# Reading two weight matrices in wide halves instead of quarters while expert rows stream in

## The chip, the core and the metric

The kernel runs on one core of one Trainium2 chip. The metric is the device time of one execution in microseconds (us), lower is better. Time before: 3602.56 us, the median of 3 runs (3600.56 to 3604.57).

## What is computed

Two layers of an encoder over 256 tokens of width 2048, all in float32. Layer 0 mixes tokens with latent attention, layer 1 with attention that has a forget gate (`fox`). After each mixer comes an expert layer (PEER): 8 query heads pick 16 experts each out of 16384 by two lists of 128 keys, so 128 expert rows of `u` and 128 of `v` (8 KB each) are fetched for every token.

```
def fox_mixer(h, w_in, b_f, g_q, g_k, w_o):
    z = h @ w_in                                   # 2048 x (4*2048 + 16)
    q, k, v, gate, f_logit = split(z)
    ...                                            # attention, 16 heads of 128
    return (o * sigmoid(gate)) @ w_o               # 2048 x 2048
def peer_ffn(h, w_q, sub_keys, u, v):
    q = x @ w_q                                    # 2048 x 2048
    scores = einsum('thcd,cnd->thcn', q, sub_keys)
    ...                                            # top 16 of each list, top 16 of the sums, softmax g
    a = gelu(einsum('tkd,td->tk', u[idx], x)) * g
    return einsum('tk,tkd->td', a, v[idx])
```

## The kernel before, in words

**Slots and windows.** The expert layer is a stream of 512 slots. One slot serves 128 tokens with one expert each: it gathers 128 rows of `u` and 128 rows of `v` (1 MB each). 128 slots are a window: window 0 and 1 are layer 0's token blocks 0 and 1, window 2 and 3 those of layer 1. For slot n, GpSimd (POOL) issues the gathers (L672 for `u`, L682 for `v`), VectorE (DVE) forms the dot products (L1967), ScalarE (ACT) applies gelu and gate and builds a diagonal matrix (L1396, L1400, L1405), TensorE (PE) adds `diag @ v` for 1536 columns to three PSUM banks (`accumulate`, L981) and DVE does the last 512 columns (L1978). `u` and `v` have a ring of 4 buffers each; a buffer is gathered into again when the slot four before is through.

**Jobs inside the slots.** Layer 1's mixer and the expert queries of layer 1, for one token block, are a "job" that is spread over the slots of a window: job 0 runs in window 1, job 1 in window 2. The place of every step is a slot number written out by hand; in each slot an engine first does the slot's expert work and then, in program order, what `job(b, at)` lists for that slot. All engines wait in order, so a step that has to wait holds up the engine's next slots.

**Weights in a job.** SyncE (SP) loads 98 pieces of 1 MB per job into a ring of 4 buffers (`stage`, taken in turn): a gain row, 64 pieces of the input matrix `fox_w_in`, 16 of the output matrix `fox_w_o`, a gain row, 16 of the query matrix `peer_w_q`. SP issues piece m when piece m-4 has been used (`staged`, L583). For the input matrix a piece is an *eighth*: 256 rows by 1024 columns (`stage_wide`, L601, so 4096 bytes of each row), and PE sums 1024 columns at once into banks 3 and 4 (`in_eighth`, L1033, matmuls L1045), one eighth per slot from slot 6 to 69. For `fox_w_o` and `peer_w_q` a piece is a *quarter*: 512 rows by 512 columns (`stage_quarter`, L597, 2048 bytes of each row), summed into one bank (`gemm_quarter`, L1024, matmuls L1030).

**Order around the change.** The output projection has four column tiles of four quarters, placed by `OUT_ORDER` at slots 70 to 73, 79 to 83, 85 to 91; a quarter needs the transposed attention outputs of its four heads (`ot_done`). Tile t is added to the residual by DVE one slot after its last quarter (`out_add`, L2071). At slot 93 (`FFN_AT`) ACT squares the residual, DVE normalises at 94 (`b_norm`, L1990; it uses the gain row and waits for its load), PE transposes at 95 and 96, ACT copies at 96 and 97. From slot 98 (`PQ_AT`) to 113 the 16 quarters of `peer_w_q` are summed, tiles alternating between banks 3 and 4; ACT copies tile i four slots after its start (`pq_copy`, L1543), PE transposes it, ACT copies that (L1550), PE multiplies by the keys, ACT stores the scores (L1556, last at slot 118). The first reader of the scores is DVE at slot 121 (`choose`, which waits for the first tile alone).

Of the kernel before, what the change touches and what calls it, by code (L numbers as in the profile page):

```python
# [26 lines left out]
ALU = mybir.AluOpType  # L27
# [7 lines left out]
P = 128  # L35
# [109 lines left out]
def hybrid_encoder(nc, x, positions, norm_mix_g, norm_ffn_g, mla_w_in, mla_g_qa, mla_w_qb, mla_g_kva,  # L145
                   mla_w_kvb, mla_g_q, mla_g_k, mla_w_o, fox_w_in, fox_b_f, fox_g_q, fox_g_k, fox_w_o,
                   peer_w_q, peer_sub_keys, peer_u, peer_v, inv_freq, out):
    with ExitStack() as ctx:
# [295 lines left out]
        def out_summed(job, t):  # L444
            return after(job, M_OUT + OUT_LOADS.index((t, 3)))

        def pq_summed(job, i):
            return after(job, M_PQ + 4 * i + 3)
# [31 lines left out]
        def _(sp):  # L480
# [114 lines left out]
            def stage_quarter(job, m, w, q, c0):  # L595
                r = staged(job, m)
                sp.dma_start(stage[:, r], w[:, 4 * q:4 * q + 4, c0:c0 + TILE]).then_inc(stage_full[r], 16)  # L597

# [102 lines left out]
        def _(pe):  # L701
# [283 lines left out]
            def b_transposes(b, ffn, quads):  # L985

                pe.wait_ge(bn_done, 2 * b + ffn + 1)
                if not ffn and quads[0] == 0:
                    if b == 0:

                        pe.wait_ge(match_done, PHEADS)
                    else:

                        pe.wait_ge(pq_evac, 4 * b)
                        pe.wait_ge(score_done, 4 * b)
                if ffn and quads[0] == 0:

                    pe.wait_ge(out_added, 4 * (b + 1))
# [25 lines left out]
            def gemm_quarter(job, m, q, bank, src):  # L1024

                r, turn = stage_of(job, m)
                pe.wait_ge(stage_full[r], 16 * (turn + 1))
                for c in range(4):
                    k = 4 * q + c
                    last = pe.matmul(psum[:, bank, :], src[:, k, :], stage[:, r, c, :], start=k == 0, stop=k == KC - 1)  # L1030
                last.then_inc(stage_used, 1)

            def in_eighth(b, i, e):  # L1033


# [4 lines left out]
                r, turn = stage_of(b, M_IN + 8 * i + e)  # L1040
                pe.wait_ge(stage_full[r], 16 * (turn + 1))
                for c in range(2):
                    k = 2 * e + c
                    for half in range(2):
                        last = pe.matmul(psum[:, 3 + half, :], b_xT[:, k, :], wide(r)[:, c, half * TILE:(half + 1) * TILE],  # L1045
                                         start=k == 0, stop=k == KC - 1)
                last.then_inc(stage_used, 1)
# [58 lines left out]
            def out_quarter(b, t, q):  # L1106

                if q == 0:
                    if t < 2:
                        pe.wait_ge(in_evac, 8 * b + 8)  # L1110
                    elif t == 2:
                        pe.wait_ge(s_masked, HEADS * (b + 1))
                    else:
                        pe.wait_ge(og_done, HEADS * (b + 1))
                pe.wait_ge(ot_done, HEADS * b + 4 * q + 4)
                gemm_quarter(b, M_OUT + OUT_LOADS.index((t, q)), q, OUT_BANKS[t], b_attnT)

            def pq_quarter(b, i, q):

                if q == 0 and i < 2:  # L1120
                    pe.wait_ge(bt_done, 8 * b + 8)
                elif q == 0:
                    pe.wait_ge(pq_evac, 4 * b + i - 1)
                gemm_quarter(b, M_PQ + 4 * i + q, q, 3 + i % 2, b_xT)

            def pq_turned(b, i):

                number = 4 * b + i
                pe.wait_ge(pq_evac, number + 1)
                if i:  # L1130
                    pe.wait_ge(pqt_done, number)
                for c in range(4):
                    last = transpose(psum[:, 5, c * P:(c + 1) * P], b_v[:, c * P:(c + 1) * P])
                last.then_inc(pqt_full, 1)
# [12 lines left out]
            def job(b, at):  # L1147
# [25 lines left out]
                if at in OUT_ORDER:  # L1173
                    out_quarter(b, *OUT_ORDER[at])
                if FFN_AT + 2 <= at < FFN_AT + 4:
                    b_transposes(b, 1, range(2 * (at - FFN_AT - 2), 2 * (at - FFN_AT - 1)))
                for i in range(4):
                    if at == PQ_AT + 4 * i + 5:
                        pq_turned(b, i)
                    if at == PQ_AT + 4 * i + 7:  # L1180
                        pq_scores(b, i)
                if PQ_AT <= at < PQ_AT + 16:
                    pq_quarter(b, (at - PQ_AT) // 4, (at - PQ_AT) % 4)
# [27 lines left out]
        def _(act):  # L1211
# [235 lines left out]
            def b_square(b, ffn):  # L1447

                if ffn:
                    act.wait_ge(out_added, 4 * (b + 1))  # L1450
# [87 lines left out]
            def pq_copy(b, i):  # L1538

                number = 4 * b + i  # L1540
                act.wait_ge(stage_used, pq_summed(b, i))
                act.wait_ge(pqt_full, number)
                nc.scalar.activation(b_v[:, 0:TILE], psum[:, 3 + i % 2, :], ACT.Copy).then_inc(pq_evac, 1)  # L1543
# [14 lines left out]
            def job(b, at):  # L1558
# [28 lines left out]
                if FFN_AT + 3 <= at < FFN_AT + 5:  # L1587
                    b_copies(b, 1, range(2 * (at - FFN_AT - 3), 2 * (at - FFN_AT - 2)))
                for i in range(4):
                    lag = at - (PQ_AT + 4 * i)  # L1590
                    if lag == 4:
                        pq_copy(b, i)
                    if lag == 6:
                        pq_turned(b, i)
                    if lag == 8:
# [40 lines left out]
        def _(dve):  # L1636
# [430 lines left out]
            def out_add(b, t):  # L2067

                dve.wait_ge(stage_used, out_summed(b, t))
                cols = resid[:, b, t * TILE:(t + 1) * TILE]  # L2070
                V.tensor_tensor(cols, psum[:, OUT_BANKS[t], :], cols, ALU.add).then_inc(out_added, 1)  # L2071

            def job(b, at):
# [22 lines left out]
                if OUT_ORDER.get(at - 1, (0, 0))[1] == 3:  # L2096
# [57 lines left out]
```

## Time and profile before

| what | value |
|---|---|
| median of the runs | 3602.56 us |
| the profiled execution, its own time | 3597.09 us |
| span of the profile (first to last instruction) | 3595.0 us |
| mean granted TensorE clock | 0.913 of full |
| busy: PE, DVE, ACT, POOL | 80%, 57%, 26%, 41% of the span |
| bytes moved | 1345.35 MB, 374 GB/s over the span |
| of them gathers (POOL's queue) | 1073.81 MB |
| of them SP's loads | 269.99 MB |

The profiled execution is 5.5 us under the median. Times in all views are from the start of the span. "DMA share" is the mean busy share of the core's 16 DMA engines; packets of two queues overlap a little, so a full queue reads 1.01 to 1.02. In the wait views the name before the arrow is the engine that sat idle, the one behind it the work that ended the wait; "issue" is idle time for which the profile shows no releaser. "Us to landing" is the time from SP's or POOL's issue of a transfer to its last byte.

### The profile page before, as it was taken

To read this page: it belongs to the slowest core of one execution; us is meant where nothing else is said; L and a number is where in the kernel's file an instruction comes from. 1 tells how busy PE (TensorE), PEld (TensorE's weight loads), DVE (VectorE), ACT (ScalarE), POOL (GpSimd) and SP (SyncE) were. 2 spreads that over 40 slices of the span, in tenths; PEclk is the share of its full clock that TensorE was granted. 3 is DMA by queue.
4 is the path that set the end of the run, shared out by engine and by line. 5 is a ranking of instruction groups with operands and counts; after the bars stand their busy time and mean duration, and the time that the engine had idled before them with its cause. 6 is when DMAs were issued, how large, how long until landed. Compare 5 with 4: busy or idle time off the path is not lost.

```text
span 3595.0 us, 26702 instructions
## 1 busy us (share of the span) xinstructions
PE 2877.5 (80%) x7322; PEld 1355.1 (38%) x7322; DVE 2034.9 (57%) x3584; ACT 945.4 (26%) x2349; POOL 1456.3 (41%) x1065
## 2 busy tenths in 40 slices
PE   7888977777786888888788788998988867776766
PEld 6445743333332433333333233443433322222222
DVE  2333156666667554555464655455546467677765
ACT  3334322222222223323221222332322122222221
POOL 4002545555655322222343532322234355555554
PEclk8877988898998999999998899999999988888888
DMA  4212599999999999999999999999999989999998
GB/s 144 82 61 89 195 386 416 416 412 415 418 419 421 418 417 417 417 417 413 409 406 400 408 418 417 417 417 417 413 412 410 400 362 421 421 421 421 422 420 360
DMA packets 262853, 1345.35 MB, mean 374 GB/s; under 512 B 27200, under 2 KB 48192, under 8 KB 130368
## 3 DMA queue, kind: packets, MB, share of 16 engines
q0 software_dynamic: 147456, 1073.81, 72.2%
q1 hardware_dynamic: 115264, 269.99, 19.9%
q8 instruction: 56, 0.92, 0.1%
q14 instruction: 77, 0.63, 0.0%
HBM read 1341.62 MB, written 2.10 MB: 374 GB/s over the span
## 4 chain that ended last, share of the span: by engine, by line
DMA 61%; PE 20%; issue 12%; POOL 3%; DVE 2%; ACT 1%; SPq 1%; DVEq 0%; POOLq 0%; ACTq 0%
DMA room<-in_peer_v_dram,index 51%; PE psum L981 11%; DMA wbuf<-in_fox_w_o_dram 5%; DMA wbuf<-in_peer_w_q_dram 4%; PE psum L1030 2%; PE psum L1045 2%; POOL room L672 1%; PE psum L744 1%; PE psum L745 1%; PE psum L746 1%; POOL room L682 1%; DMA room<-in_peer_u_dram,index 1%; DVE resid L1978 0%; SPq L539 0%; POOL w_low L656 0%
## 5 line engine op out<-in xcount | busy, mean ns | idle before, releaser
L981 PE MATMUL psum<-room,diag 128*128 128x512 f32 x3072 | 1605.6, 664 | 554.2 <-DMA room<-in_peer_v_dram,index 493.9
L1967 DVE CUSTOM_DVE_ANT_0 room<-room,normed 128x2048 f32<-128x2048 f32 x512 | 1172.8, 2291 | 613.7 <-DMA room<-in_peer_u_dram,index 609.4
L682 POOL DMA_INDIRECT room<-in_peer_v_dram,index x512 | 749.4, 1464 | 1083.3 <-PE psum L981 1050.1
L981 PEld LDWEIGHTS psum<-room,diag 128*128 128x128 f32 x3072 | 603.6, 208 | 1497.0 <-issue 1239.8
L672 POOL DMA_INDIRECT room<-in_peer_u_dram,index x512 | 590.7, 1154 | 729.5 <-DVE dots L1967 482.4
L1396 ACT ACTIVATE acts<-dots 128x1 f32<-128x1 f32 x512 | 103.4, 202 | 1765.6 <-DVE dots L1967 1765.2
L1978 DVE SCALAR_TENSOR_TENSOR resid<-room,acts,resid 128x512 f32<-128x512 f32 x512 | 384.2, 750 | 306.6 <-DMA room<-in_peer_v_dram,index 236.8
L1045 PE MATMUL psum<-wbuf,normedT 128*128 128x512 f32 x1024 | 463.6, 595 | 0.0
L1030 PE MATMUL psum<-wbuf,normedT 128*128 128x512 f32 x512 | 272.4, 682 | 83.4 <-DMA wbuf<-in_peer_w_q_dram 41.8
L1045 PEld LDWEIGHTS psum<-wbuf,normedT 128*128 128x128 f32 x1024 | 188.9, 190 | 214.7 <-issue 212.0
L656 POOL TENSOR_TENSOR w_low<-wbuf,w_high 128x2048 fp32r<-128x2048 f32 (+1 forms) x28 | 113.9, 4080 | 304.4 <-ACT w_high L1251 304.4
L1405 ACT ACTIVATE diag<-ident,acts 128x128 f32<-128x128 f32 x512 | 205.5, 401 | 48.3 <-ACT acts L1400 1.5
L1030 PEld LDWEIGHTS psum<-wbuf,normedT 128*128 128x128 f32 x512 | 108.5, 219 | 225.0 <-issue 183.6
L1400 ACT ACTIVATE acts<-acts,gates 128x1 f32<-128x1 f32 x512 | 150.8, 295 | 16.6
L873 PE MATMUL psum<-wbuf,room 128*128 128x384 f32 (+1 forms) x256 | 119.4, 605 | 0.7 <-ACT room L1283 0.7
L920 PE MATMUL psum<-normedT,wbuf 128*128 128x256 f32 x448 | 106.0, 379 | 0.0
L920 PEld LDWEIGHTS psum<-normedT,wbuf 128*128 128x128 f32 x448 | 85.5, 191 | 36.5 <-issue 27.8
L1396 ACT ACT_TABLE_LOAD x74 | 94.9, 1283 | 1.3
L706 PE MATMUL psum<-ident,room 128*128 128x128 f32 x192 | 46.6, 341 | 31.8 <-DVE room L1714 14.0
L1251 ACT ACTIVATE w_high<-wbuf 128x2048 fp32r<-128x2048 f32 (+1 forms) x28 | 47.5, 1702 | 80.6 <-DMA wbuf<-in_mla_w_o_dram 52.1
L873 PEld LDWEIGHTS psum<-wbuf,room 128*128 128x128 f32 x256 | 50.8, 216 | 37.8 <-issue 30.1
L1811 DVE CUSTOM_DVE_ANT_0 room<-psum,mask_mla 128x128 f32<-128x128 f32 (+1 forms) x32 | 11.5, 358 | 93.8 <-PE psum L816 91.9
(199 smaller groups left out, 1800.8 us busy)
## 6 DMA issues: line engine op xcount, KB each, us to landing
wbuf<-in_fox_w_in_dram SPq DMA_DIRECT2D x128, 1024.0 KB, 12.5
wbuf<-in_fox_w_o_dram SPq DMA_DIRECT2D x32, 1024.0 KB, 31.9
wbuf<-in_peer_w_q_dram SPq DMA_DIRECT2D x32, 1024.0 KB, 28.2
wbuf<-in_mla_w_o_dram SPq DMA_DIRECT2D x16, 1024.0 KB, 5.1
wbuf<-in_peer_w_q_dram SPq DMA_DIRECT2D x32, 512.0 KB, 9.1
wbuf<-in_mla_w_in_dram SPq DMA_DIRECT2D x8, 1024.0 KB, 8.3
wbuf<-in_mla_w_kvb_dram SPq DMA_DIRECT2D x32, 256.0 KB, 3.4
room<-in_peer_u_dram,index POOLq DMA_INDIRECT x512, 16.6
```

The costliest lines, as they stand in the source:

```text
L672: pool.indirect_dma_start(u_ring[:, r, :], None, u_table, bass.IndirectOffsetOnAxis(index[:, number % 2, s:s + 1], 0)).then_inc(u_full[r], 16)
L682: pool.indirect_dma_start(v_ring[:, r, :], None, v_table, bass.IndirectOffsetOnAxis(index[:, number % 2, s:s + 1], 0)).then_inc(v_full[r], 16)
L873: last = pe.matmul(gbank(gh, b)[:, 0:n], (cqT, ckvT)[t][:, k, b * P:(b + 1) * P], wbuf[:, wh, k, 0:n], start=k == 0, stop=k == RC - 1)
L920: last = pe.matmul(psum[:, 4 + c, 0:T], pq_tile[:, r, k, c * P:(c + 1) * P], normedT[:, k, :], start=k == 0, stop=k == KC - 1)
L981: mm = pe.matmul(psum[:, q, :], diag[:, r, :], v_ring[:, r, q * TILE:(q + 1) * TILE], start=at == 0, stop=at == WINDOW - 1, skip_group_che ...
L1030: last = pe.matmul(psum[:, bank, :], src[:, k, :], stage[:, r, c, :], start=k == 0, stop=k == KC - 1)
L1045: last = pe.matmul(psum[:, 3 + half, :], b_xT[:, k, :], wide(r)[:, c, half * TILE:(half + 1) * TILE], start=k == 0, stop=k == KC - 1)
L1396: chain.step(nc.scalar.activation(acts[:, 0, r:r + 1], dots[:, r:r + 1], ACT.Gelu))
L1400: chain.step(nc.scalar.activation(acts[:, 1, r:r + 1], acts[:, 0, r:r + 1], ACT.Copy, scale=gates[:, number % 2, s:s + 1]))
L1405: nc.scalar.activation(diag[:, r, :], ident[:, :], ACT.Copy, scale=acts[:, 1, r:r + 1]).then_inc(diag_ready, 1)
L1967: V.tensor_tensor_reduce(u_ring[:, r, :], u_ring[:, r, :], normed[:, b, :], 1.0, 0.0, ALU.mult, ALU.add, dots[:, r:r + 1]).then_inc(dot_do ...
L1978: V.scalar_tensor_tensor(out=resid[:, b, PE_COLS:D], in0=v_ring[:, r, PE_COLS:D], scalar=acts[:, 1, r:r + 1], in1=resid[:, b, PE_COLS:D], ...
```

## The change

The 32 quarters of a job become 32 eighths, as the input matrix has them: 256 rows by 1024 columns, still 1 MB each, in eight steps per half of the matrix. The output projection's first half sums into banks 3 and 4, its second into 5 and 6. A half is added to the residual by one DVE instruction of 1024 columns; the two query halves both use banks 3 and 4, each copied by one ACT instruction of 1024 columns, and the transposes read that copy in two parts of 512 columns. The order is written anew: output eighths at slots 70 to 73, 79, 80, 83, 85 to 93; the norm and the queries start two slots later.

```diff
-FFN_AT = 93
-PQ_AT = 98
-OUT_ORDER = {70: (0, 0), 71: (0, 1), 72: (1, 0), 73: (1, 1), 79: (0, 2), 80: (1, 2), 81: (2, 0), 82: (2, 1),
-             83: (2, 2), 85: (3, 0), 86: (3, 1), 87: (0, 3), 88: (1, 3), 89: (2, 3), 90: (3, 2), 91: (3, 3)}
-OUT_BANKS = (3, 4, 6, 5)
+FFN_AT = 95
+PQ_AT = 100
+OUT_ORDER = {70: (0, 0), 71: (0, 1), 72: (0, 2), 73: (0, 3), 79: (0, 4), 80: (0, 5), 83: (0, 6), 85: (1, 0),
+             86: (1, 1), 87: (0, 7), 88: (1, 2), 89: (1, 3), 90: (1, 4), 91: (1, 5), 92: (1, 6), 93: (1, 7)}
+OUT_BANKS = (3, 5)
+def pq_at(i):
+    return PQ_AT + 8 * (i // 2) + 2 * (i % 2)
...
-                for m, (t, q) in enumerate(OUT_LOADS):
-                    stage_quarter(job, M_OUT + m, ow, q, t * TILE)
+                for m, (half, e) in enumerate(OUT_LOADS):
+                    stage_wide(job, M_OUT + m, ow, e, half * WIDE)
                 stage_gain(job, M_FFN, norm_ffn_g[1:2, :])
-                for t in range(4):
-                    for q in range(4):
-                        stage_quarter(job, M_PQ + 4 * t + q, qw, q, t * TILE)
+                for half in range(2):
+                    for e in range(8):
+                        stage_wide(job, M_PQ + 8 * half + e, qw, e, half * WIDE)
...
-            def gemm_quarter(job, m, q, bank, src):
+            def gemm_eighth(job, m, e, bank, src):
                 r, turn = stage_of(job, m)
                 pe.wait_ge(stage_full[r], 16 * (turn + 1))
-                for c in range(4):
-                    k = 4 * q + c
-                    last = pe.matmul(psum[:, bank, :], src[:, k, :], stage[:, r, c, :], start=k == 0, stop=k == KC - 1)
+                for c in range(2):
+                    k = 2 * e + c
+                    for half in range(2):
+                        last = pe.matmul(psum[:, bank + half, :], src[:, k, :], wide(r)[:, c, half * TILE:(half + 1) * TILE],
+                                         start=k == 0, stop=k == KC - 1)
                 last.then_inc(stage_used, 1)
...
+            def out_eighth(b, half, e):
+                if e == 0 and half == 0:
+                    pe.wait_ge(in_evac, 8 * b + 8)
+                elif e == 0:
+                    pe.wait_ge(s_masked, HEADS * (b + 1))
+                    pe.wait_ge(og_done, HEADS * (b + 1))
+                pe.wait_ge(ot_done, HEADS * b + 2 * e + 2)
+                gemm_eighth(b, M_OUT + OUT_LOADS.index((half, e)), e, OUT_BANKS[half], b_attnT)
+            def pq_eighth(b, half, e):
+                if e == 0 and half == 0:
+                    pe.wait_ge(bt_done, 8 * b + 8)
+                elif e == 0:
+                    pe.wait_ge(pq_evac, 2 * b + 1)
+                gemm_eighth(b, M_PQ + 8 * half + e, e, 3, b_xT)
...
+            def pq_copy(b, half):
+                act.wait_ge(stage_used, pq_summed(b, half))
+                act.wait_ge(pqt_full, 4 * b + 2 * half)
+                nc.scalar.activation(b_v, psum[:, 3:5, :].rearrange("p k n -> p (k n)"), ACT.Copy).then_inc(pq_evac, 1)
...
+            def out_add(b, half):
+                dve.wait_ge(stage_used, out_summed(b, half))
+                cols = resid[:, b, half * WIDE:(half + 1) * WIDE]
+                bank = OUT_BANKS[half]
+                V.tensor_tensor(cols, psum[:, bank:bank + 2, :].rearrange("p k n -> p (k n)"), cols,
+                                ALU.add).then_inc(out_added, 1)
```

In the new order PE transposes query part i at slot `pq_at(i) + 9` and multiplies it by the keys at +11; ACT copies a half at `PQ_AT + 8 * half + 8`, the transposed part at `pq_at(i) + 10` and the scores at +12 (slots 112, 114, 120, 122). `in_eighth` now calls `gemm_eighth` with the same matmuls as before. The other waits on `out_added` and `pq_evac` count two per job instead of four.

## Rows read from the trace of the kernel before

**Rows 1.** The page: DMA share (tenths) and rate, span in 40 slices.

```profile
DMA  4212599999999999999999999999999989999998
GB/s 144 82 61 89 195 386 416 416 412 415 418 419 421 418 417 417 417 417 413 409 406 400 408 418 417 417 417 417 413 412 410 400 362 421 421 421 421 422 420 360
```

**Rows 2.** Busy time, clock, DMA share and rate in stretches; first row names columns.

```profile
core 0: us, PE busy (x) PEld busy (x) DVE busy (x) ACT busy (x) POOL busy (x), PEclk, DMA share, GB/s
1190.00:1630.00 440.00, 381.46 (x943) 165.40 (x942) 230.31 (x443) 120.12 (x272) 115.47 (x117) 1.00 1.02 417
...
1640.00:1990.00 350.00, 289.12 (x681) 127.44 (x680) 181.44 (x297) 91.96 (x224) 121.93 (x96) 0.92 1.01 407
2540.00:2900.00 360.00, 305.86 (x761) 139.22 (x760) 189.90 (x308) 97.25 (x235) 133.60 (x100) 0.93 0.99 394
2980.00:3560.00 580.00, 408.23 (x693) 148.72 (x694) 407.90 (x607) 125.02 (x376) 324.14 (x232) 0.85 1.01 421
1792.00:1800.00 8.00, 6.97 (x15) 2.73 (x14) 5.33 (x16) 0.90 (x3) 1.93 (x2) 0.89 0.93 333
1928.00:1936.00 8.00, 8.00 (x20) 3.54 (x20) 5.64 (x6) 1.56 (x6) 3.85 (x2) 0.85 0.84 315
2828.00:2836.00 8.00, 8.00 (x20) 3.48 (x18) 5.67 (x6) 1.52 (x5) 3.77 (x2) 0.79 0.81 303
2884.00:2892.00 8.00, 8.00 (x19) 3.48 (x18) 3.49 (x4) 2.17 (x7) 2.27 (x1) 0.87 0.01 4
```

**Rows 3.** DMA queues, 1210 to 1620 us (eighths load): packets, MB, share of 16 engines.

```profile
q0 software_dynamic: 15632, 113.84, 66.9%
q1 hardware_dynamic: 14782, 57.01, 34.7%
```

**Rows 4.** DMA queues, 1650 to 1780 us (quarters load).

```profile
q0 software_dynamic: 5684, 41.38, 77.1%
q1 hardware_dynamic: 6161, 12.23, 25.0%
```

**Rows 5.** Line 1978, once a slot: 1190-1630, 1725-1770, 1838-1890, 2980-3560 us (count; durations; first, last start).

```profile
L1978 DVE SCALAR_TENSOR_TENSOR resid<-room,acts,resid x58: 746/752/753, 1191.0 to 1626.6; 128x512 f32<-128x512 f32 x58
...
L1978 DVE SCALAR_TENSOR_TENSOR resid<-room,acts,resid x7: 752/752/753, 1726.6 to 1765.2; 128x512 f32<-128x512 f32 x7
...
L1978 DVE SCALAR_TENSOR_TENSOR resid<-room,acts,resid x9: 750/752/753, 1838.3 to 1889.8; 128x512 f32<-128x512 f32 x9
...
L1978 DVE SCALAR_TENSOR_TENSOR resid<-room,acts,resid x116: 745/751/753, 2981.5 to 3558.6; 128x512 f32<-128x512 f32 x116
```

**Rows 6.** The page's DMA issues: count, KB each, median us to landing.

```profile
wbuf<-in_fox_w_in_dram SPq DMA_DIRECT2D x128, 1024.0 KB, 12.5
wbuf<-in_fox_w_o_dram SPq DMA_DIRECT2D x32, 1024.0 KB, 31.9
wbuf<-in_peer_w_q_dram SPq DMA_DIRECT2D x32, 1024.0 KB, 28.2
```

**Rows 7.** Who waited for whom, whole span: us in total, times, longest us.

```profile
DVE resid L1978 <- issue: 68.9, 8, 18.8
...
DVE resid L2071 <- PE psum L1030: 50.2, 6, 22.1
```

**Rows 8.** Timeline around 2880 us: start, us, engine, line, operation, idle before.

```profile
2880.33 6.54 PE L1030 MATMUL psum<-wbuf,normedT 128*128 128x512 f32 x8 [4.70 <-DMA wbuf<-in_peer_w_q_dram]
...
2886.91 0.60 ACT L1543 ACTIVATE wbuf<-psum 128x512 f32<-128x512 f32 x1 [10.64 <-PE psum L1030]
...
2889.72 2.55 POOL L682 DMA_INDIRECT room<-in_peer_v_dram,index  x1 [12.26 <-PE psum L981]
```

**Rows 9.** Single lines: count, duration ns min/median/max, first and last start.

```profile
L1484 ACT ACTIVATE share<-psum x8: 1024/1024/1027, 1236.7 to 2441.7; 128x1024 f32<-128x1024 f32 x8
...
L1543 ACT ACTIVATE wbuf<-psum x8: 597/597/601, 1876.8 to 2886.9; 128x512 f32<-128x512 f32 x8
...
L2071 DVE TENSOR_TENSOR resid<-psum,resid x8: 680/692/693, 1794.6 to 2719.8; 128x512 f32<-128x512 f32 x8
```

More of the change, by code:

```diff
@@ L442, in in_summed, with out_summed, pq_summed @@
             return after(job, M_IN + 8 * i + 7)
[L444 to L448, printed above, removed]
+        def out_summed(job, w):
+            return after(job, M_OUT + OUT_LOADS.index((w, 7)))
+        def pq_summed(job, w):
+            return after(job, M_PQ + 8 * w + 7)
         def psum_tile(n):
@@ L992, in b_transposes @@
                     else:
-                        pe.wait_ge(pq_evac, 4 * b)
+                        pe.wait_ge(pq_evac, 2 * b)
                         pe.wait_ge(score_done, 4 * b)
                 if ffn and quads[0] == 0:
-                    pe.wait_ge(out_added, 4 * (b + 1))
+                    pe.wait_ge(out_added, 2 * (b + 1))
                 for q in quads:
@@ L1039, in in_eighth @@
                     pe.wait_ge(in_evac, 8 * b + i)
[L1040 to L1047, printed above, removed]
+                gemm_eighth(b, M_IN + 8 * i + e, e, 3, b_xT)
             def qk_turned(b, g, kind, half):
@@ L1104, in out_turned @@
                 transpose(psum[:, 7, T:T + P], b_og[:, :]).then_inc(ot_full, 1)
[L1106 to L1120, printed above, removed]
+            def out_eighth(b, half, e):
[8 more added lines that the diff above has]
+                if e == 0 and half == 0:
                     pe.wait_ge(bt_done, 8 * b + 8)
-                elif q == 0:
-                    pe.wait_ge(pq_evac, 4 * b + i - 1)
-                gemm_quarter(b, M_PQ + 4 * i + q, q, 3 + i % 2, b_xT)
+                elif e == 0:
+                    pe.wait_ge(pq_evac, 2 * b + 1)
+                gemm_eighth(b, M_PQ + 8 * half + e, e, 3, b_xT)
             def pq_turned(b, i):
                 number = 4 * b + i
-                pe.wait_ge(pq_evac, number + 1)
+                pe.wait_ge(pq_evac, 2 * b + i // 2 + 1)
                 if i:
@@ L1132, in pq_turned @@
                 for c in range(4):
-                    last = transpose(psum[:, 5, c * P:(c + 1) * P], b_v[:, c * P:(c + 1) * P])
+                    at = i % 2 * TILE + c * P
+                    last = transpose(psum[:, 5, c * P:(c + 1) * P], b_v[:, at:at + P])
                 last.then_inc(pqt_full, 1)
@@ L1173, in job @@
                 if at in OUT_ORDER:
-                    out_quarter(b, *OUT_ORDER[at])
+                    out_eighth(b, *OUT_ORDER[at])
                 if FFN_AT + 2 <= at < FFN_AT + 4:
@@ L1177, in job @@
                 for i in range(4):
-                    if at == PQ_AT + 4 * i + 5:
+                    if at == pq_at(i) + 9:
                         pq_turned(b, i)
-                    if at == PQ_AT + 4 * i + 7:
+                    if at == pq_at(i) + 11:
                         pq_scores(b, i)
                 if PQ_AT <= at < PQ_AT + 16:
-                    pq_quarter(b, (at - PQ_AT) // 4, (at - PQ_AT) % 4)
+                    pq_eighth(b, (at - PQ_AT) // 8, (at - PQ_AT) % 8)
             def peer():
@@ L1449, in b_square @@
                 if ffn:
-                    act.wait_ge(out_added, 4 * (b + 1))
+                    act.wait_ge(out_added, 2 * (b + 1))
                 else:
@@ L1536, in out_copy @@
                 nc.scalar.activation(b_attnT[:, h, :], psum[:, 7, T:T + P], ACT.Copy).then_inc(ot_done, 1)
[L1538 to L1543, printed above, removed]
+            def pq_copy(b, half):
+                act.wait_ge(stage_used, pq_summed(b, half))
+                act.wait_ge(pqt_full, 4 * b + 2 * half)
+                nc.scalar.activation(b_v, psum[:, 3:5, :].rearrange("p k n -> p (k n)"), ACT.Copy).then_inc(pq_evac, 1)
             def pq_turned(b, i):
@@ L1588, in job @@
                     b_copies(b, 1, range(2 * (at - FFN_AT - 3), 2 * (at - FFN_AT - 2)))
+                for half in range(2):
+                    if at == PQ_AT + 8 * half + 8:
+                        pq_copy(b, half)
                 for i in range(4):
[L1590 to L1593, printed above, removed]
+                    if at == pq_at(i) + 10:
                         pq_turned(b, i)
-                    if lag == 8:
+                    if at == pq_at(i) + 12:
                         pq_scores(b, i)
@@ L2095, in job @@
                             qk_norm(b, g, kind)
-                if OUT_ORDER.get(at - 1, (0, 0))[1] == 3:
+                if OUT_ORDER.get(at - 1, (0, 0))[1] == 7:
                     out_add(b, OUT_ORDER[at - 1][0])
```

7 lines of the change are left out of this document (removed).

## The prediction, made before the changed kernel ran

> **What bounds the kernel now.** I read the page's DMA slices first [rows 1]: from the sixth slice to the end nearly all stand at 9, so the expert stream is bound by bytes, and no engine's busy time matters as long as the DMA engines have work. The rate, though, isn't the same everywhere: 417 in the slices where the input matrix is read, 421 where only gathers run, but 413, 409, 406, 400, 408 (slices 19 to 23) and 413, 412, 410, 400, 362 (29 to 33) where the output matrix and the queries are read. Next the table by stretch [rows 2]: 407 GB/s in job 0's part that the change touches (1640 to 1990 us), 394 in job 1's (2540 to 2900), against 417 in the stretch of eighths. The reader is to see two things: these two stretches move the same kind of bytes at a lower rate, and a few short holes in them, the largest at 2884 to 2892 us where the rate is 4 GB/s.
>
> Why lower? The queues answer [rows 3, 4]. Gather packets and load packets come about one to one in both stretches (15632 to 14782, 5684 to 6161), so a queue's share of the rate goes by the size of its packets. With 4096-byte rows the loads get 57.01 of 170.9 MB, 139 GB/s, which is one 1.05 MB piece in 7.5 us; a slot takes (1626.6-1191.0)/57 = 7.64 us [rows 5], so one piece per slot is just what comes. With 2048-byte rows they get 12.23 MB in 130 us, 94 GB/s, one piece in 11.1 us, while slots go by in 38.6/6 = 6.43 and 51.5/8 = 6.44 us [rows 5] and each wants a piece. The ring of four empties, a piece lands 28 to 32 us after its issue where an eighth takes 12.5 [rows 6], and all engines stand at the next step that needs the tile's end, until the gather rings are full, no gather is left, and the loads have the DMA engines alone. DVE's share of these stands is 68.9 + 50.2 us [rows 7]. Most of this costs nothing, as DMA keeps moving; what costs is the hole when the loads are through and the gathers have not restarted. The end of job 1 shows it [rows 8]: PE starts on the last piece at 2880.33 and takes 6.54 us (the granted clock of that stretch is 0.87, the 2.4 GHz level with part of it at 1.2 [rows 2]), ACT had waited 10.64 us for it, and POOL's next gather is issued at 2889.72. No load of a next job fills in there, so nothing moves.
>
> **The change part by part.**
>
> *Bytes and instructions.* Still 98 pieces of 1 MB per job, the same SP issues, the same number of matmuls with the same 512 columns and weight loads. Nothing for SP, POOL and PE.
>
> *Packets.* 64 pieces, 67.1 MB, go from 2048 to 4096 bytes. DMA time per MB of loads: 0.250 x 130/12.23 = 2.657 us before [rows 4], 0.347 x 410/57.01 = 2.496 us with wide rows [rows 3]. Difference 0.161 x 67.1 = 10.8 us, over a share of 1.02: 10.6 us. The Trainium skill, DMA: Bandwidth & Descriptors, "Why small descriptors are slow (HBM only)", gives a fixed cost of about 3 cycles per packet of 32-byte beats; by it 67/64 against 131/128 cycles is 2.3%, an estimate of 3.7 us on these bytes, and the gain below would be 21 us instead of 28. I follow the rows, which have the kernel's own traffic at 6%. No row shows 4096-byte packets out of these two matrices; the nearest are `fox_w_in`'s (2.496 us/MB) and the gathers' 8 KB ones (0.669 x 410/113.84 = 2.41), and at the other end the narrow ones. So the term lies between 0 and 0.25 x 67.1/1.02 = 16 us; I take 10.6, by the rows of the same width.
>
> *Holes.* At 2884 to 2892 the whole 8 us is lost; at 1792 to 1800, 1928 to 1936 and 2828 to 2836 it is 8 x (1 - 333/417), (1 - 315/417) and (1 - 303/417): 1.6 + 2.0 + 2.2 [rows 2]. Together 13.8 us. They go if pieces land one per slot, as for the input matrix, whose stretch holds 417 GB/s throughout. The new order asks for at most one per slot: nine in a row (85 to 93) and sixteen (100 to 115), with free slots ahead of both in which the ring fills. The last piece is issued after slot 111 and lands 12.5 us later [rows 6], two slots on, for slot 115.
>
> *The sum by rates.* 350 x (1 - 407/417) = 8.4 us and 360 x (1 - 394/417) = 19.9 us: 28.3 us. Packets and named holes make 24.4 of it; the other 4 are patches where loads run alone. The upper bound is the rate of gathers alone, 421: 11.6 + 23.1 = 34.7.
>
> *Later steps.* Norm, queries and scores move two slots back, the last scores to slot 122. The first reader at 121 wants the first tile, written at 112; the others are read in the next window. Next job's first transposes stand at its slot 3, nine slots on. Nothing; if it did hold, it would be a slot or so, 5 us.
>
> *New wait.* The second query half uses the same banks, so PE at slot 108 waits for ACT's copy of the first. Behind it stand PE's eighth and the next `accumulate`, and POOL's `v` gather waits for that. The input matrix has this handoff every eight slots (copy 1.02 us [rows 9]) at 417 GB/s, so the rings cover it: nothing; without cover 1 to 2 us, twice. The copies themselves: 8 x 0.597 against 4 x 1.024 on ACT, 8 x 0.692 on DVE against 4 of at most 1.4 [rows 9], both off the bound. The second half's first eighth at slot 85 needs the last head's output of slot 84, as tile 3 had.
>
> Sum: 3597.1 - 28.3 = 3568.8 us for an execution like the profiled one. The median of the runs is 5.5 us higher, so 3574.3.
>
> **Rivals.**
> *The rate stays, only holes go.* What decides the rate would be the size of a transfer, which stays 1024 KB, not of a packet; then 28.3 - 10.6 = 17.7 us: 3584.9. Against it: 6% between rows 3 and 4 at equal transfer size. The Trainium skill, same page, "Bandwidth", advises batching to 1 MiB, which both versions have; by that rule alone the width changes nothing.
> *The end of job 1 still pauses.* No next job there, and a chain PE, ACT, diagonal, PE, POOL must restart, so the 8 us stay: 3582.3. For it: the chain is untouched. Against: it only opens since the last piece is late.
> *Slower: the stands stay, the pace falls.* The loads' share grows, so the 32 slots of a job that read a piece go from 6.44 to 7.64 us: 2 x 32 x 1.20 = +77 us. That is repaid by the 119 us of DVE's stands [rows 7] only if these are really waits for weights. If they come from the chain of norm, copies and scores, they stay. It decides from the point where over a third stays; with half, 77 - 60 = +17: 3619.6. Against it: the loads' landing times, and that DMA was full during most of the stands, so that bytes can't take longer unless holes grow.
> *The rows aren't read wider.* Should the DMA cut rows to 2048 bytes anyway, nothing changes: 3602.6. Against: the count of packets in rows 3, 57.01 MB in 14782.
>
> **How the numbers follow.** Forecast 0.74, rate stays 0.10, pause stays 0.09, no effect 0.03, slower 0.04. A measurement of this kernel can tell about 0.2%, 7.2 us, from no change. Faster: the first three, 0.93; same 0.03; slower 0.04. The range takes in both rivals of a smaller gain (3584.9) and 3 us for the runs' own spread above; below, the bound of 34.7 us (3567.9) and the same 3: 3565 to 3588.
>
> **What would show it.** In the profile after: GB/s of about 417 in slices 19 to 23 and 29 to 33, none under 410; median landing of `fox_w_o` and `peer_w_q` near 12.5 to 15 us; slots with a piece at 7.6 us and none of 20 us or more; PE's waits for these loads gone and its clock nearer 1.00; DVE's line 1978 and the residual add with a few us of waits in place of 119; no hole after job 1's last piece. The forecast is wrong if the rate in those slices stays under 413, if POOL still waits over 10 us at the end of job 1, or if slots lengthen with the stands in place.

## The result and the profile after

| | before | after |
|---|---|---|
| median of 5 runs | 3602.06 us (3600.56 to 3604.57) | 3583.42 us (3579.43 to 3585.38) |
| ratio, 95% interval | | 0.9948 (0.9934 to 0.9962) |
| profiled execution, its own time | 3597.09 us | 3579.43 us |
| span | 3595.0 us | 3577.5 us |
| mean granted TensorE clock | 0.913 | 0.917 |

Faster by 18.7 us by the ratio (13.7 to 23.8), 17.5 us by the two spans. The forecast was 28.3 us, so the direction and the place were right, and two thirds of the size came. One execution of all those timed for this document, one of stand30, took 5326 us and is left out of its ratio.

The page's DMA lines after the change, which answer to [rows 1]:

```profile
DMA  4212599999999999999999999999999999999998
GB/s 145 83 62 81 194 384 416 416 414 417 416 417 422 418 417 417 417 417 418 416 419 417 413 417 417 417 417 417 416 400 419 417 408 418 418 417 420 415 417 357
```

The reader is to see that slices 19 to 22 now stand at 416 to 419 where they were at 400 to 413, but also three things that the forecast didn't have: 400 in slice 30, where the kernel before had 412, 408 in slice 33, and 415 to 420 in slices 34 to 39, where the kernel before had 420 to 422. The same by stretch (columns as in [rows 2]):

```profile
1190.00:1630.00 440.00, 381.56 (x943) 165.34 (x942) 230.83 (x442) 119.92 (x272) 115.70 (x116) 1.00 1.02 417
1640.00:1990.00 350.00, 286.88 (x683) 124.48 (x682) 187.78 (x302) 92.96 (x226) 118.96 (x101) 0.94 1.02 417
2540.00:2900.00 360.00, 306.59 (x771) 137.78 (x770) 206.05 (x338) 99.57 (x239) 130.47 (x109) 0.95 1.01 413
...
1928.00:1936.00 8.00, 6.99 (x20) 3.15 (x19) 3.05 (x3) 1.49 (x4) 1.88 (x2) 1.00 1.02 420
2604.00:2612.00 8.00, 6.64 (x20) 3.52 (x21) 6.33 (x11) 4.60 (x10) 2.33 (x3) 1.00 0.90 334
2866.00:2874.00 8.00, 8.00 (x20) 3.49 (x19) 4.66 (x4) 1.47 (x4) 3.08 (x3) 1.00 1.00 401
...
2909.00:2914.00 5.00, 3.31 (x4) 1.51 (x5) 3.12 (x4) 0.90 (x3) 4.09 (x3) 0.66 0.87 310
2884.00:2892.00 8.00, 6.30 (x23) 3.56 (x24) 5.87 (x16) 2.77 (x8) 5.66 (x4) 1.00 1.02 428
```

Job 0's stretch is at the forecast 417. The hole behind job 1's last piece, at 2884 to 2892 in the kernel before, is gone: that piece is now read by PE at 2868.77, with 401 GB/s from 2866 to 2874, and 2884 to 2892 is at 428. New small holes are at 2604 to 2632 (334 GB/s to 2612, then 379) and where the windows change, 2909 to 2914.

The queues where the queries of job 0 are read, 1905 to 1950 us: packets, MB, share of 16 engines, to be held against [rows 4]:

```profile
q0 software_dynamic: 1686, 12.28, 65.7%
q1 hardware_dynamic: 1681, 6.49, 36.1%
```

Again one load packet to one gather packet, but the load's share is now 6.49 of 18.77 MB, 144 GB/s, a piece in 7.3 us. The Trainium skill, DMA: Bandwidth & Descriptors, "Queues, rings and completion order", says that each DMA engine takes turns between its queues packet by packet; the two counts agree with it, though the page's packet holds some 9 to 17 descriptors and the packets counted here are one row each, so that they show equal numbers and not how many rows make a turn.

The waits of DVE, total, times, longest, against [rows 7]:

```profile
DVE resid L2067 <- PE psum L1033: 23.5, 4, 6.6
...
DVE resid L1973 <- issue: 1.4, 1, 1.4
```

24.9 us in place of 119.1. The end of job 1's queries in the timeline (start, us, engine, line), which answers to [rows 8]:

```profile
2863.20 2.36 POOL L683 DMA_INDIRECT room<-in_peer_v_dram,index  x1 [1.19 <-PE psum L982]
...
2868.77 3.60 PE L1033 MATMUL psum<-wbuf,normedT 128*128 128x512 f32 x8
...
2872.41 1.02 ACT L1538 ACTIVATE wbuf<-psum 128x1024 f32<-128x1024 f32 x1 [6.59 <-PE psum L1033]
```

PE waits for no load here, takes 3.60 us for the piece instead of 6.54, and POOL, which waited 12.26 us here before, waits at most 3.8 us from 2855 to 2900 us. The longest slot behind slot 130 is 11.1 us, where it was 25.7. The pace of the slots is line 1973's (1190 to 1630, then 2980 to 3560 us), which answers to [rows 5]:

```profile
L1973 DVE SCALAR_TENSOR_TENSOR resid<-room,acts,resid x58: 746/752/754, 1191.5 to 1627.2; 128x512 f32<-128x512 f32 x58
...
L1973 DVE SCALAR_TENSOR_TENSOR resid<-room,acts,resid x115: 746/751/815, 2984.1 to 3556.0; 128x512 f32<-128x512 f32 x115
```

571.9/114 = 5.017 us per slot in the gather-only stretch, where the kernel before had 577.1/115 = 5.018: the rate there fell from 421 to 418 GB/s and the slots didn't notice. The rate in 40 slices of 14 us, 2980 to 3540 us, before and then after the change:

```profile
GB/s 422 422 418 422 424 423 421 421 420 422 422 419 422 421 420 422 421 420 422 422 421 421 421 421 422 421 421 421 422 422 422 420 421 421 420 421 417 421 422 421
```

```profile
GB/s 420 396 426 420 422 422 399 417 422 422 421 422 401 411 422 421 421 422 409 422 422 422 421 421 401 422 420 424 421 401 412 422 421 421 421 397 424 422 421 421
```

After the change seven slices fall to 396 to 409; before it none is under 417. By the starts of line 1973's instructions most slots take 4.95 to 4.98 us, which for their 2.097 MB is 422 GB/s; but once in 16 slots, where the head changes, two take 6.0 and 6.6 us and the next 2.9, in both kernels. The mean of 5.017 us, 418 GB/s, comes from that. At these places the gathers run ahead of the slots: by 1.5 slots before the change, with the rate unbroken, and by 2.4 after it, where the rate falls, to 363 and 389 GB/s at 2994 to 3002 us. That the four buffers of a ring are then all full or under way is argued, not shown. That the rate here follows the slots, and not the slots the rate, is the clue to the third that is missing.

### The profile page after: what moved, and what is told of

The parts are those of the page before. It is cut to its first block, busy times and chain, and to the rows that moved or that the text cites. A ratio compares the mean times of both kernels' runs of the same rounds, so it can differ in the third digit from the quotient of the medians.

```text
span 3577.5 us, 26686 instructions
## 1 busy us (share of the span) xinstructions
PE 2869.6 (80%) x7322; PEld 1347.5 (38%) x7322; DVE 2037.9 (57%) x3580; ACT 946.3 (26%) x2345; POOL 1422.9 (40%) x1065
## 4 chain that ended last, share of the span: by engine, by line
DMA 64%; PE 20%; issue 11%; DVE 3%; POOL 1%; ACT 1%; SPq 1%; DVEq 0%; POOLq 0%; ACTq 0%
DMA room<-in_peer_v_dram,index 64%; PE psum L982 12%; PE psum L1033 3%; PE psum L745 1%; PE psum L746 1%; PE psum L747 1%; POOL room L673 1%; DVE room L1962 0%; DVE resid L1973 0%; POOL room L683 0%; DMA room<-in_peer_u_dram,index 0%; SPq L544 0%; POOL w_low L657 0%; SPq L514 0%; PE psum L948 0%
## 5 line engine op out<-in xcount | busy, mean ns | idle before, releaser
L982 PE MATMUL psum<-room,diag 128*128 128x512 f32 x3072 | 1636.2, 675 | 628.1 <-DMA room<-in_peer_v_dram,index 581.6
L673 POOL DMA_INDIRECT room<-in_peer_u_dram,index x512 | 558.3, 1090 | 757.9 <-DVE dots L1962 529.6
L1033 PE MATMUL psum<-wbuf,normedT 128*128 128x512 f32 x1536 | 695.1, 595 | 0.0
L1033 PEld LDWEIGHTS psum<-wbuf,normedT 128*128 128x128 f32 x1536 | 285.3, 191 | 330.7 <-issue 327.6
L921 PEld LDWEIGHTS psum<-normedT,wbuf 128*128 128x128 f32 x448 | 85.5, 191 | 36.5 <-issue 27.8
L745 PE MATMUL psum<-w_high,other 128*128 128x512 f32 x128 | 50.9, 398 | 4.5 <-issue 4.5
```

Of the source, the lines that this page charges most:

```text
L673: pool.indirect_dma_start(u_ring[:, r, :], None, u_table, bass.IndirectOffsetOnAxis(index[:, number % 2, s:s + 1], 0)).then_inc(u_full[r], 16)
L921: last = pe.matmul(psum[:, 4 + c, 0:T], pq_tile[:, r, k, c * P:(c + 1) * P], normedT[:, k, :], start=k == 0, stop=k == KC - 1)
L982: mm = pe.matmul(psum[:, q, :], diag[:, r, :], v_ring[:, r, q * TILE:(q + 1) * TILE], start=at == 0, stop=at == WINDOW - 1, skip_group_che ...
L1033: last = pe.matmul(psum[:, bank + half, :], src[:, k, :], wide(r)[:, c, half * TILE:(half + 1) * TILE], start=k == 0, stop=k == KC - 1)
```

## The experiments

All are edits of the changed kernel, timed in 5 rounds beside the kernel before. "Against the change" is the difference of the two ratios to the kernel before, times 3602 us; from the two intervals, taken as independent, each carries some 6 to 7 us of uncertainty either way. So +20, +27 and +21 are clear of it, +9 and +10 too, +7 just, and +5 is not.

| run | median us | ratio to before (95%) | against the change |
|---|---|---|---|
| the change | 3583.42 | 0.9948 (0.9934 to 0.9962) | |
| w_split | 3580.94 | 0.9951 (0.9937 to 0.9964) | +1 |
| n_all | 3600.26 | 1.0003 (0.9994 to 1.0012) | +20 |
| n_out | 3587.29 | 0.9967 (0.9955 to 0.9979) | +7 |
| n_last | 3591.48 | 0.9977 (0.9967 to 0.9987) | +10 |
| n_first | 3583.92 | 0.9961 (0.9947 to 0.9975) | +5 |
| n_in | 3606.74 | 1.0023 (1.0014 to 1.0032) | +27 |
| stand20 | 3589.52 | 0.9972 (0.9962 to 0.9982) | +9 |
| stand30 | 3599.59 | 1.0005 (0.9996 to 1.0015) | +21 |
| spread | 3579.98 | 0.9950 (0.9936 to 0.9963) | +1 |
| q8 | 3578.98 | 0.9946 (0.9932 to 0.9959) | -1 |
| q8_spread | 3581.74 | 0.9951 (0.9937 to 0.9964) | +1 |

### Is it the packets, or the new order? (n_all, w_split)

```diff
 def stage_wide(job, m, w, e, c0):
     r = staged(job, m)
+    if in_two(job, m):               # the run says for which pieces
+        for h in range(2):
+            sp.dma_start(stage[:, r, 2 * h:2 * h + 2, :],
+                         w[:, 2 * e:2 * e + 2, c0 + h * TILE:c0 + (h + 1) * TILE]).then_inc(stage_full[r], 16)
+        return
     sp.dma_start(wide(r), w[:, 2 * e:2 * e + 2, c0:c0 + WIDE]).then_inc(stage_full[r], 16)
```

PE reads the columns from where they then lie, and the waits on `stage_full` count both transfers. n_all does it for all 64 output and query pieces:

> The changed kernel with its order, banks and waits, but each of the 64 pieces of the output matrix and the queries is read as two transfers of 512 columns (2048-byte packets, 512 KB each) instead of one of 1024 columns. Theory (the gain is the packet width: a third instead of a fifth of the rate for the loads, and 1% more bytes per us): it gives back the whole gain, 3602 us (3598 to 3606), with landing times near 30 us, DVE standing over 100 us on line 1973 and the residual add, and a hole of about 8 us after job 1's last piece. Rival (the new order and the wide summation carry part of it): 3593 us or less, with fewer stands at packets of 2048 bytes.

The control cuts a piece in two by rows, so that transfers are 512 KB too but packets stay wide:

```diff
+        for c in range(2):
+            sp.dma_start(wide(r)[:, c, :], w[:, 2 * e + c, c0:c0 + WIDE]).then_inc(stage_full[r], 16)
```

> A control for the run with narrow packets: also two transfers of 512 KB per piece, but each is one row of 1024 columns (4096-byte packets). If packet width is what counts: within 2 us of the changed kernel (3581 to 3586), landing and stands as there. If the size of a transfer counts: towards 3590 us or more, with a lower rate in slices 19 to 23 and 29 to 33.

n_all took 3600.26 us, ratio 1.0003: the whole gain is gone, with the new order, the new banks and the wide sums all in place. Its waits of DVE:

```profile
DVE resid L1988 <- issue: 100.8, 10, 15.6
...
DVE resid L2082 <- PE psum L1049: 65.2, 4, 27.2
```

166 us of stands, more than before the change. The control kept the gain. Landing times can be read in both pages (KB, median us; the 512 KB query row also holds 32 transfers of layer 0), first w_split's:

```profile
wbuf<-in_fox_w_in_dram SPq DMA_DIRECT2D x128, 1024.0 KB, 12.5
wbuf<-in_peer_w_q_dram SPq DMA_DIRECT2D x96, 512.0 KB, 13.0
wbuf<-in_fox_w_o_dram SPq DMA_DIRECT2D x64, 512.0 KB, 11.3
```

and n_all's:

```profile
wbuf<-in_peer_w_q_dram SPq DMA_DIRECT2D x96, 512.0 KB, 15.9
wbuf<-in_fox_w_o_dram SPq DMA_DIRECT2D x64, 512.0 KB, 25.9
```

11.3 us against 25.9 for the same 512 KB of the output matrix. So the rival in which only the holes go and the rate is set by the size of a transfer falls, and the advice of the Trainium skill (same page, "Bandwidth") to batch to 1 MiB doesn't bind here: halving the transfers costs nothing that can be measured (+1 us, give or take 7). n_all's pause after job 1's last piece lies across the end of the stretch from 2540 to 2900 us, so that it is best taken by itself: from 2880 to 2910 us it has 309 GB/s, 7.8 us of bytes, about the 8 expected. The kernel before has 252 GB/s there, 11.9 us, and that is more than the 8 us that the prediction gave this hole.

### Where do narrow packets cost? (n_out, n_last, n_first, n_in)

The same edit for a part of the pieces: the output matrix alone, job 1's queries alone, job 0's alone, and the input matrix alone.

> Only the 32 pieces of the output matrix narrow, the queries wide. Theory: half the bytes (1% of rate on half the stretches, about 3 us) and the stands of the output part with small holes (2 us): 3588 us (3585 to 3592), and no hole at the end of job 1, since the queries come wide. Rival (the lag carries over into the queries): over 3593.

> Only job 1's 16 query pieces narrow. It asks what the pause at the end of job 1 is worth. By holes at full price (8 us pause, 2 us of the earlier one, 2 us of packets): +12 us, 3595. By the theory that a pause is partly made up afterwards, because the gather-only stretch of the changed kernel ran at 418 GB/s where that of the kernel before, after its pause, ran at 421: +6 to +8 us, 3590 us, and 421 GB/s in the last 500 us.

n_out came at 3587.29 us, +7, as the theory had it; its queries land in time (15.8 us, the page's median), and DVE's stands are all at the residual add of the output half (65.5 us, 4 times), none at line 1988 for want of a query. n_last came at +10 (13.9 by the spans, 3591.4 against 3577.5), nearer the full price of the holes (+12) than the +6 to +8 of the other theory, though the 6 us of uncertainty take in both. Its pause, in the timeline:

```profile
2879.82 6.55 PE L1049 MATMUL psum<-wbuf,normedT 128*128 128x512 f32 x8 [4.49 <-DMA wbuf<-in_peer_w_q_dram]
...
2892.70 1.02 ACT L1553 ACTIVATE wbuf<-psum 128x1024 f32<-128x1024 f32 x1 [20.92 <-PE psum L1049]
...
2894.73 0.75 DVE L1988 SCALAR_TENSOR_TENSOR resid<-room,acts,resid 128x512 f32<-128x512 f32 x1 [16.79 <-issue]
```

But the other theory's sign was there all the same, two of its stretches reading

```profile
2540.00:2900.00 360.00, 304.05 (x740) 136.34 (x740) 191.96 (x304) 94.74 (x229) 129.21 (x101) 0.91 0.98 393
2960.00:3540.00 580.00, 406.90 (x695) 147.77 (x694) 408.18 (x607) 125.01 (x376) 324.73 (x231) 0.85 1.01 421
```

393 GB/s where the change has 413, then 421 where it has 418. What this means, the next group shows.

> The counterpart of the run with job 1's queries narrow: now only job 0's 16 query pieces are narrow, the same bytes in the same steps. Behind them stand the next job's loads, so DMA has work while the engines stand. If a stand costs only where DMA runs dry: packets alone (16.8 MB x 0.161 us = 2.7 us) and holes of 1 to 2 us: +3 to +5 us over the changed kernel, 3587, with stands of 15 us and more all the same. If a stand costs by itself: as much as in job 1, +10 us, 3594.

n_first: +5 by the ratio, +1.0 by the spans (3578.5 against 3577.5), for the same bytes as n_last. Its stands are as long. The timeline at the two ends of query halves, ACT and then DVE:

```profile
1931.89 1.02 ACT L1553 ACTIVATE wbuf<-psum 128x1024 f32<-128x1024 f32 x1 [26.73 <-PE psum L1049]
...
1992.46 1.02 ACT L1553 ACTIVATE wbuf<-psum 128x1024 f32<-128x1024 f32 x1 [22.37 <-PE psum L1049]
```

```profile
1933.92 0.75 DVE L1988 SCALAR_TENSOR_TENSOR resid<-room,acts,resid 128x512 f32<-128x512 f32 x1 [17.10 <-issue]
...
1994.48 0.75 DVE L1988 SCALAR_TENSOR_TENSOR resid<-room,acts,resid 128x512 f32<-128x512 f32 x1 [17.00 <-issue]
```

ACT idle for 22 to 27 us, DVE for 17, twice. What the DMA engines did at these two ends (n_first) and at job 1's last one (n_last; columns as in [rows 2]):

```profile
1925.00:1945.00 20.00, 18.88 (x41) 8.36 (x42) 7.83 (x8) 4.77 (x14) 7.42 (x4) 0.86 0.85 311
1985.00:2005.00 20.00, 19.49 (x57) 9.37 (x56) 8.80 (x9) 5.79 (x16) 10.56 (x6) 1.00 1.02 417
```

```profile
2880.00:2900.00 20.00, 19.98 (x43) 8.73 (x44) 5.27 (x5) 3.98 (x11) 6.06 (x4) 0.86 0.57 215
```

The first stand of n_first, with only the second half's own narrow pieces behind it, costs 20 x (1 - 311/417) = 5.1 us of bytes. The second, with job 1's loads behind it in the queue, costs none. In n_last, where nothing stands behind, the same wait costs 20 x (1 - 215/417) = 9.7 us. So it is what lies in the queue that decides, not the stand. The two runs as a whole say it less sharply: by the ratios they differ by 6 us, with 6 of uncertainty. By the spans it is 13, but 5.1 of that lies at 2594 to 2683 us, with 417 GB/s in n_first and 393 in n_last, ahead of any piece that either edit touches; the change has 400 there. So the +1.0 of n_first holds 3.6 us of gain that its edit has no part in, and without them it agrees with the +5 of the ratio.

> Only the 128 pieces of the input matrix narrow (two transfers of 512 columns), output and queries wide. The loads now get a fifth of the rate for 64 slots in a row, so pieces come late all the time and every handoff to ACT is a stand; but DMA always has loads queued. If bytes at their packets' price are what counts: 134.2 MB x 0.161 = 21.6 us, and 3 to 10 us of holes: 3608 to 3616. If the stands cost by themselves, 16 handoffs at 15 us or more beyond that: over 3640.

n_in: +27 us by the ratio (24.1 by the spans), 21.6 of which the packets' price gives for its 134.2 MB; its median is just under the range expected, 3606.74 us against 3608 to 3616. The stands are the longest list of all, and the rate says where the time is:

```profile
DVE resid L1988 <- issue: 127.5, 18, 15.0
...
ACT share L1495 <- PE psum L1049: 85.3, 8, 25.2
```

```profile
1190.00:1630.00 440.00, 379.89 (x907) 170.05 (x907) 223.12 (x437) 115.41 (x266) 135.59 (x114) 0.93 1.02 405
...
2100.00:2520.00 420.00, 372.35 (x932) 170.65 (x931) 217.16 (x431) 113.44 (x255) 125.84 (x108) 0.95 1.02 402
```

DMA share 1.02, so never dry, at 405 and 402 GB/s. 440 x (1 - 405/417) + 420 x (1 - 402/417) = 27.8 us. This is the cleanest price for the width of packets: 24 to 28 us on 134.2 MB, 0.18 to 0.21 us per MB, which the 6 us of uncertainty don't tell from the 0.161 of the forecast. By the fixed cost per packet that the Trainium skill states (same page, "Why small descriptors are slow (HBM only)"), an estimate of 2.3% or 7 us, it would have been under a third of that; the measurement decides.

### What is a hole worth? (stand20, stand30)

```diff
+if b == 1 and at == 124:
+    for _ in range(20):              # 30 in stand30
+        chain.step(nc.scalar.activation(b_v, psum[:, 3:5, :].rearrange("p k n -> p (k n)"), ACT.Copy))
+        chain.settle()
```

> The changed kernel with a bare stand added: at slot 124 of job 1's window ACT makes 20 idle copies of 1.02 us one after another, 21 us in all; nothing else changes. It prices a stand whose engines wait but whose gathers go on. Both rings hold four slots, so up to some 16 to 20 us of gathers can land meanwhile: a hole of 1 to 5 us in the DMA traffic. If only the hole costs: +1 to +5 us over the changed kernel, 3586 us. If the whole stand costs: +21 us, 3604.

> The same with 30 copies, 31 us. The hole must be some 10 us longer than with 20. If a hole costs its full length: +10 us over the run with 20 copies, 3596. If part of it is made up in the gather-only stretch behind it (421 GB/s there in the kernel before, 418 in the changed one): +5 to +7 us over the run with 20 copies, and 421 GB/s from 2960 to 3540 us.

A stand of 21 us cost 9 (10.8 by the spans), more than the 1 to 5 expected of the hole alone and far from the 21 of the whole stand. The next 10 us cost 12 by the ratios, 10.1 by the medians and 9.2 by the spans: the rings cover some 10 to 12 us, and beyond them a hole costs its full length, not the half that one of the expectations offered. The stretches 2900 to 2960 and 2960 to 3540 us, stand20 and then stand30:

```profile
2900.00:2960.00 60.00, 32.58 (x64) 12.84 (x63) 35.25 (x45) 32.81 (x55) 26.34 (x20) 0.79 0.79 314
2960.00:3540.00 580.00, 414.59 (x694) 147.63 (x693) 408.50 (x607) 124.77 (x376) 318.25 (x232) 0.84 1.01 421
```

```profile
2900.00:2960.00 60.00, 25.82 (x50) 10.14 (x50) 27.38 (x37) 40.35 (x56) 15.95 (x14) 0.72 0.61 239
2960.00:3540.00 580.00, 410.44 (x696) 147.25 (x696) 409.93 (x609) 125.04 (x376) 323.93 (x233) 0.84 1.01 421
```

Against the change, which has 408 and 418 there, stand20 is short of 94 x 60 = 5.6 MB in the first stretch, 13.5 us at 418 GB/s, and its span is 10.8 us longer; stand30 of 169 x 60 = 10.1 MB, 24.3 us, and its span is 20.0 us longer. That is 2.7 and 4.3 us less than the bytes say, and each time there are 3 GB/s more for 580 us afterwards: 1.7 MB, or 4.2 us. So the bytes that are missing after a stand come in two kinds. One is time: DMA idle. The other is **lead**: rows that have landed before their slot needs them.

The lead can be counted in the traces: 8192-byte gather packets landed when line 1973's instruction (1978, 1977 in the others) starts for the 401st time, in MB, less the 401 x 2.097 = 841.0 MB that so many slots use. The gather queue has then moved 845.1 MB in the change, 843.0 in the kernel before and 842.7 in stand20. In slots that is a lead of 1.9, 0.9 and 0.8. For the 496th, 95 slots later, it is 1.7, 1.6 and 1.5. So a long pause takes about one slot's rows (2.1 MB) from the rings, that loss delays no slot, and most of it is refilled at 421 GB/s while slots go on at 5.017 us in either case. The rate of the last stretch goes by the lead at its start in every run: 421 GB/s where it is 0.7 to 0.9 slots (before, n_all, n_last, stand20, stand30), 420 at 1.2 (n_out, which has no pause just ahead), 419 at 1.7 (n_in), 417 and 418 at 1.8 and more.

### Small steps further (spread, q8, q8_spread)

```diff
-OUT_ORDER = {70: (0, 0), 71: (0, 1), 72: (0, 2), 73: (0, 3), 79: (0, 4), 80: (0, 5), 83: (0, 6), 85: (1, 0),
+OUT_ORDER = {70: (0, 0), 72: (0, 1), 74: (0, 2), 76: (0, 3), 78: (0, 4), 80: (0, 5), 83: (0, 6), 85: (1, 0),
```

> The changed kernel, but the first five output pieces stand at slots 70, 72, 74, 76, 78 instead of 70 to 73 and 79, then 80, 83 and the rest as before. It is to close the small holes of job 1 at slots 74 to 79 (about 2605 to 2632 us: 405 GB/s in a stretch in which no piece is loaded and PE's matmuls fall to half pace). If these holes come from having no piece to load there: 1 to 3 us less, 3581. If they come from the chain of the last heads (softmax, table loads): the same within 1 us, and the holes stay.

The hole at 2604 to 2612 us shrank (spread's row, to be held against the 334 GB/s above):

```profile
2604.00:2612.00 8.00, 8.00 (x25) 3.96 (x24) 3.51 (x6) 0.90 (x3) 2.14 (x2) 1.00 0.97 372
2540.00:2900.00 360.00, 302.81 (x774) 136.42 (x773) 207.20 (x340) 99.47 (x241) 130.62 (x110) 0.97 1.01 414
```

but the stretch is at 414 instead of 413 and the time the same. (The expectation puts 2605 to 2632 us of the change at 405 GB/s; the view has 366.) Which of the two causes the hole has stays open: slice 30 went from 400 to 408 GB/s, 1.7 us, too little to be measured in the time. And the same slice has 417 GB/s from 2594 to 2683 us in n_first, which reads job 1's pieces just as the change does, so that the hole comes and goes without any edit there.

```diff
+def pq_row(b, k):
+    ...
+    for n in range(4):
+        last = pe.matmul(psum[:, 3 + n, :], b_xT[:, k, :], stage[:, r, n, :], start=k == 0, stop=k == KC - 1)
```

> The next step of the same idea, for the queries alone: a piece is 128 rows of all 2048 columns (8192-byte packets), 16 steps into four banks, both halves copied at slot 116, the last scores at slot 126. If width goes on paying as by the time per MB of loads (2.496 at 4096 bytes, 2.41 at 8192): 33.6 MB x 0.086 = 2.9 us at most, half of it by the rate of the narrow step; 3581 us (3580 to 3584). If the later scores or the four-bank copy at one slot open a hole: 3586 or more.

> Both small steps together: queries in rows of 8 KB and the first five output pieces spread over slots 70 to 78. The spread one had its hole at 2605 to 2632 us shrunk (408 instead of 400 GB/s in slice 30) with no gain clear of noise, the other was 4 us under the changed kernel by medians, inside the intervals. Together 3578 us (3575 to 3582) if the two add up; anything from 3580 to 3584 says that they are noise.

q8's medians and ratio are the lowest of all (3578.98 us, 0.9946) but not clear of the change's interval, and the two together gave 0.9951. No version beats the change by what can be measured.

## Why the prediction was right in direction and too large by half

*What bounds the kernel.* Right where loads run. The loads' share went by the packets (rates and counts above), n_all undid the gain by packet width alone. In the gather-only stretch it is right between two changes of head, 4.97 us per slot at 422 GB/s; what a change of head adds, under 1 us in 16 slots, isn't bytes.

*The number alone.* It doesn't speak for the forecast: 3583.42 us is nearer the rival with only the holes (3584.9) than the 3574.3 forecast. What decides for the packets are the rates, w_split and n_in. That the measured gain (18.7 us) comes so near the gain of the holes alone (17.7) is luck: packets paid about as forecast, and the lead and the new holes took as much away.

*Packets, 10.6 us.* About right: n_in's 24 to 28 us on 134.2 MB is 12 to 14 us on 67.1 MB. The estimate of 3.7 us, which the prediction worked out from the Trainium skill (DMA: Bandwidth & Descriptors, "Why small descriptors are slow (HBM only)"), is too low, and the rival with nothing for the rate falls.

*Holes, 13.8 us.* The four named ones went, and the end of job 1 doesn't pause, so that rival falls too. The last one was larger than the 8 us taken for it: the kernel before has 172 GB/s from 2880 to 2900 us, 11.7 us of bytes. Missed: I took no new ones in their place. They are at 2604 to 2632 us, 1.6 + 1.8 = 3.4 us, and at 2909 to 2914 where the windows change, 1.3 us. With pieces on time no load lags into slots 74 to 79 of job 1, and DMA has only gathers there; that this, or the chain of the last heads, opens the first of them is argued, not shown, and job 0's slots 74 to 79 have no such hole (416 GB/s in slice 20). PE's rows in the timeline of the changed kernel, two slots in turn just ahead:

```profile
2589.81 2.81 PE L982 MATMUL psum<-room,diag 128*128 128x512 f32 x6 [0.51 <-DMA room<-in_peer_v_dram,index]
...
2597.51 5.46 PE L982 MATMUL psum<-room,diag 128*128 128x512 f32 x6 [3.42 <-DMA room<-in_peer_v_dram,index]
```

The same six matmuls take twice as long. The granted clock from 2597 to 2603 us is 0.50, the 1.2 GHz level, behind a wait of 3.42 us. From 2604 to 2612 it is 1.00 again, and that the slow matmuls deepen the hole is argued, not shown.

*The sum by rates, 28.3 us: this step failed.* I wrote "360 x (1 - 394/417) = 19.9 us" and called the 4 us beyond the named parts "patches where loads run alone"; 3.7 of them are the rest of the hole behind job 1's last piece. By the stretches of the change it goes: 8.4 us in job 0 as forecast; in job 1 360 x (1 - 413/417) = 3.5 us less, all of it in the new hole at 2604 to 2632; between 2900 and 2960 the kernel before had 421 GB/s, the change 408 (1.9 us, 1.3 of it the hole at 2909 to 2914); over 2960 to 3540 us 421 and 418 (4.2 us). 28.3 - 3.5 - 1.9 - 4.2 = 18.7 us, against 17.5 by the spans and 18.7 by the ratio. Both kernels move the same bytes, so such a sum has to close; it says where the time lies. Why is said by the counted lead and the stands: a low rate in one stretch was partly a loan that the kernel before paid back in the next, some 4 to 5 us, and I counted all of it as lost. The other 5 us are the new holes. The parts alone, 24.4 us less 4.7 of new holes, would have been nearer, but by luck: they leave out both the lead and 3.7 us of a hole, which nearly cancel.

*The signs.* By its own sign the forecast is partly wrong: slices 30 and 33 stand at 400 and 408, under the 413 that was to be the limit, and under 410. The other two signs of being wrong, POOL's long wait and longer slots with the stands in place, didn't appear. Median landing times of whole pieces don't stand in the changed kernel's page; in n_last the output matrix, wide as in the change, has 12.6 us.

*New wait, later steps.* Nothing, as forecast: around PE's handoff at slot 108 of job 0 the queues move 18.77 MB in 45 us (1905 to 1950), 417 GB/s, and the last scores are in time.

*The slower rival.* Its first half happened, the query slots with a piece went from 6.4 to 7.7 us, and its second did not: the stands fell from 119.1 to 24.9 us. n_first shows why its sum would have been wrong even so: two stands of 17 us cost some 5 us, packets included.

## What to carry to other kernels

Where two queues keep the DMA engines full, a stream's share goes by its packet size against the other's; compare pieces per us with what a slot asks for before moving any instruction. Count stands only where DMA runs dry: with the next job's loads queued behind, engines waited 17 us here at no cost in bytes, and at the last piece of a phase the same wait cost 9.7 us of them. And when a rate in one stretch is turned into time, look also at the stretch behind it, and count how far the landed rows are ahead of their slots at its start: bytes that only refill the rings' lead cost no time.

## What was unexpected in the hardware

- In the gather-only stretch the DMA rate can be 421 or 418 GB/s at the same pace of 5.017 us per slot, for 580 us on end. It goes by the lead at the stretch's start: 0.7 to 0.9 slots in the five profiles with 421, 1.8 and more in those with 417 or 418.
- 2048-byte packets beside 8192-byte ones cost 24 to 28 us on 134.2 MB, 7 to 9% of the loads' own time of 322 us at 417 GB/s, though the DMA share reads 1.02 in both. Gathers alone read 1.01, so a reading just over 1 doesn't need two queues, as the section "Time and profile before" has it.
